# Light experts of a top-2-of-8 MoE layer as plain fp32 matmuls on two 64-column tiles of the array

## The chip, the core and the metric

One core of a Trainium2 chip runs the whole program. The metric is the device time in microseconds (us) of one execution; the profile gives the time from the first to the last instruction (the span) of one profiled execution. TensorE (PE) multiplies and transposes, ScalarE (ACT) and VectorE (DVE) work on SBUF and on PSUM, SyncE (SP) issues nearly all DMAs. Weights are read from HBM, each byte once.

## The reference, cut to what matters

The model is a trunk of two layers with 256 tokens of width 1024. The mixers and the dense feed-forward of layer 0 stay as they are. The change is in the channel mixer of layer 1:

```
def swiglu(h, wg, wu, wd):
    return (jax.nn.silu(h @ wg) * (h @ wu)) @ wd

def moe_top2(h, router, wg, wu, wd):          # h: 256 tokens x 1024; wg, wu: 8 x 1024 x 3584; wd: 8 x 3584 x 1024
    logits = (hf @ router).astype(jnp.float32)
    top_val, top_idx = lax.top_k(logits, TOP_K)          # 2 of 8 experts for each token
    gates = jax.nn.softmax(top_val, axis=-1)
    ...                                                  # tokens sorted by expert, padded to blocks of 128
    return swiglu(xblk, wg[e], wu[e], wd[e])             # for each block; times the gate, added back to the tokens
```

Everything is fp32. With 8 experts of 3 x 1024 x 3584 weights the layer reads 352 MB.

## The kernel before

**Units.** The weights of an expert are cut into 42 units of 1 MB (128 partitions x 2048 fp32): 28 units of gate and up weights (`c` below `DOWN0`), then 14 units of down weights. They are read into a ring of `SLOTS` = 7 buffers, `ring`. SP waits until the unit 7 places earlier has been used by PE, then issues the load of the next (L1322, in `beside`).

**Hi and lo.** PE has a fast pass for fp32 data rounded to a shorter form (written fp32r). To keep the accuracy, each unit is split: ACT writes the rounded part to `w_hi` (`moe_split` of ACT, L1431), DVE writes the rest, the raw unit minus that, to `ring_lo` (`moe_split` of DVE, L1950). Both run `MOE_LEAD` = 4 units ahead of PE. A product is then made of hi x hi, hi x lo and lo x hi.

**Heavy and light experts.** The 8 experts are sorted by the number of their tokens. The heavy one of a pair has up to 128 tokens, the light one up to 64 (`LIGHT`). Four pairs are worked off. For a heavy expert the tokens are the stationary operand, 128 columns, and each 512 weights of a row are streamed three times (`product`, L570 to L572): 12 matmuls of 512 columns in a unit. For a light expert the 64 tokens stand twice in the 128 columns of the array, once as hi and once as lo (`xl_both`, `elT_both`), and each 512 weights are streamed twice, once from `w_hi` and once from `ring_lo` (L1055, L1056 in `in_unit`; L1080, L1081 in `down_unit`): 8 matmuls in a unit. The result lies in PSUM in two halves of 64 partitions that have to be added. This is done with the transposition that the hidden layer needs anyway: ACT copies 1024 columns from PSUM to SBUF (`light_take`), and PE multiplies each 128 columns with `fold`, two identities of 64 under one another (`transposed`, L1110; `light_gT` and `light_uT` call it, 14 times with four matmuls for each light expert, 13 of them in a light half and the last at the start of the next heavy half). Silu and the product of gate and up follow on the transposed data (`light_silu`, `light_gated`), and a hi/lo split of that (`light_hi`, `light_rest`).

**Order.** The order is written out by hand. A pair has two halves of 42 units. In the heavy half (`heavy_up`) two units of the gate and up weights of the heavy expert are followed by one down unit of the light expert before it; in the light half (`light_up`) two gate and up units of the light expert are followed by one down unit of the heavy one. The first heavy half has only its 28 heavy units. After the last light half come 14 down units of the last light expert (`light_down`), and then the rest of the layer. Within the halves lie the gathering of tokens (`gather`, L988), transposes of the heavy hidden layer (`heavy_hidden`, L1104) and the scattering of results to the tokens (`scatter`, L995, plain fp32), each at a fixed unit.

The lines that the steps of the prediction touch are L570 to L572, L1055, L1056, L1080, L1081 and L1110 on PE, L1431 on ACT, L1950 on DVE and L1322 on SP.

Of the kernel before, what the change touches and what calls it, by code (L numbers as in the profile page):

```python
# [36 lines left out]
P = 128  # L37
# [56 lines left out]
PAIR_UNITS = 2 * EXPERT_UNITS  # L94

# [23 lines left out]
def trunk(nc, params, x, p, positions, w_in, w_uq, w_ukv, w_out, dense_g, dense_u, dense_d, router,  # L119
          moe_g, moe_u, moe_d, ple_g, ple_p, final_g, out):  # L120
    with ExitStack() as ctx:
# [48 lines left out]
        class View:  # L170
# [83 lines left out]
        xl = xT_r[:, 0:KT * 2 * LIGHT].rearrange("p (k r s) -> p k r s", k=KT, r=2)  # L254
        xl_both = [xl[:, kt].rearrange("p r s -> p (r s)") for kt in range(KT)]
        vx = View(xT_b, KT * 2 * LIGHT, 2 * NT * D)
        sgT, hx = vx(8 * LIGHT), vx(8 * LIGHT)
        light_y = vx(D)
        el_at1 = vx.at
        el_at0 = vf.at  # L260
        el_at3 = el_at0 + 16 * LIGHT
        vf.at = el_at3 + 8 * LIGHT
        light_selgT, fold = vf(NT * P), vf(LIGHT)

        elT = [buf[:, at:at + 2 * n * LIGHT].rearrange("p (k r s) -> p k r s", k=n, r=2) for buf, at, n in (
            (arena_b_r, el_at0, 8), (xT_r, el_at1, 8), (small_r, 0, 8), (arena_b_r, el_at3, 4))]
        elT_both = [elT[kt // 8][:, kt % 8].rearrange("p r s -> p (r s)") for kt in range(FKT)]
# [60 lines left out]
        moe_x_hi, heavy_h_hi, light_h_hi = sem("moe_x_hi"), sem("heavy_h_hi"), sem("light_h_hi")  # L328
# [26 lines left out]
        class Banks:  # L355
# [35 lines left out]
        sgT_ready, uT_full, hx_ready = (sem(n) for n in ("sgT_ready", "uT_full", "hx_ready"))  # L391
        selgT_full, selgT_ready = sem("selgT_full"), sem("selgT_ready")
        gT_full, lT_free = sem("gT_full"), sem("lT_free")
        hT_full, hT_free, d_full, ysb_ready, sc_full, sc_free, xg_full, xg_free, consts_ready = (sem(n) for n in (
            "hT_full", "hT_free", "d_full", "ysb_ready", "sc_full", "sc_free", "xg_full", "xg_free",
            "consts_ready"))

        MOE_USED = EXPERT_UNITS - len(GROUP_ENDS)
        HT_FILLS = FKT // 4
        SCATTER = (4, 7, 4, 7)  # L400
        LAST_SCATTER = (4, 7, 0, 1)


        def position(k, c):


            up, half = c < DOWN0, EXPERT_UNITS if (c < DOWN0) == (k == 1) else 0
            return half + (c // 2 * 3 + c % 2 if up else 3 * (c - DOWN0) + 2)

        def round_of(i, k, c):  # L410

            return i + 1 if k and c >= DOWN0 else i

        def is_start(i, k, c):

            return isinstance(i, int) and i == 0 and k == 0 and c < DOWN0

        def counted_used(k, c):

            return sum(1 for kk in range(2) for cc in range(EXPERT_UNITS)  # L420
                       if position(kk, cc) <= position(k, c) and cc not in GROUP_ENDS)

        START_USED = sum(1 for c in range(DOWN0) if c not in GROUP_ENDS)

        def ch_done(i, k, ch):
            return i * (2 * NCH) + k * NCH + ch + 1

        def hT_done(i, k, n):
            return i * (NCH if k else HT_FILLS) + n + 1
# [4 lines left out]
        def xg_done(i, k, half=0):  # L434
            return i * 3 + 2 * k + half + 1

        def d_done(i, k, half):
            return i * 4 + 2 * k + half + 1
# [8 lines left out]
        def unit_of(i, k, c):  # L447

            if is_start(i, k, c):
                return S0 + c  # L450
            return round_of(i, k, c) * PAIR_UNITS + S0 - DOWN_UNITS + position(k, c)

        def ring_of(k, c, start=False):

            return N0 + c if start else N0 - DOWN_UNITS + position(k, c)

        def tail_of(n_iter, j):

            return n_iter * PAIR_UNITS + S0 - DOWN_UNITS + j

        def after_of(n_iter, c):

            return n_iter * PAIR_UNITS + S0 + c


        def by_cols(w, c0, n=SEQ):

            return [(w.rearrange("(k p) n -> p k n", p=P)[:, :, c0:c0 + n], KT, n)]
# [52 lines left out]
        def turn(g, in_moe=False):  # L521
            return S0 + g - N0 if in_moe or g >= N0 else TURN[g]
# [4 lines left out]
        def high(g, n=UNIT, in_moe=False):  # L527
            a = turn(g, in_moe) % HIGHS * UNIT
            return w_hi[:, a:a + n]

# [13 lines left out]
        def _(pe):  # L544
# [435 lines left out]
            def gather(i, k, kt):  # L980
# [8 lines left out]
                if kt % per_bank == per_bank - 1:  # L989
                    last.then_inc(xg_full, 1)  # L990

            def scatter(k, n, b, first, final):

                t, half = divmod(n, 2)
                last = mm(psum[:, b, :], selgT[k][:, t, :], ysb[k][:, half * 512:half * 512 + 512],  # L995
                          start=first, stop=final)
                if final:
                    last.then_inc(sc_full, 1)

            def scatter_two(i, n):  # L1000
# [3 lines left out]
                if n == 0:  # L1004
                    pe.wait_ge(selgT_ready, step_done(i, 0))
                    pe.wait_ge(ysb_ready, d_done(i, 0, 1))
                elif n == 2:
                    pe.wait_ge(selgT_ready, step_done(i, 1))
                    pe.wait_ge(ysb_ready, d_done(i, 1, 1))
                if n < 2:  # L1010
                    pe.wait_ge(hT_free, hT_done(i + 1, 0, n))
                else:
                    pe.wait_ge((sgT_ready, hx_ready)[n - 2], (i + 1) * NCH + 1)
# [4 lines left out]
            def spread_gates(i, k, b=7):  # L1018

                pe.wait_ge(selg_ready, step_done(i, k))  # L1020
                if b != 7:
                    pe.wait_ge(ysb_ready, d_done(i, 0, 1))
# [1670 lines left out]
```

## Time and profile before

| | us |
|---|---|
| median of 3 runs (lowest to highest) | 1483.17 (1481.64 to 1484.45) |
| span of the profiled execution | 1481.2 |
| PE matmul, busy | 1439.9 (97%) |
| PE weight load, busy | 1190.4 (80%) |
| DVE, busy | 1216.5 (82%) |
| ACT, busy | 1026.3 (69%) |
| the 336 expert units, from the first matmul to the last | about 890 |

Busy times are sums of the records of an engine. The record of a matmul begins when it starts to stream and ends when its last result is modelled to have left the array, so records of one stream overlap: what a matmul costs in a stream is the distance between two starts, not its own length. A row of the timeline with xN joins N records. One plain fp32 matmul is two MATMUL records, an fp32r matmul is one. An "idle before" in square brackets is time in which that engine had nothing running, and the name behind the arrow is what ended it.

### The profile page before, as it was taken

To read this page: it belongs to the slowest core of one execution; us is meant where nothing else is said; L and a number is where in the kernel's file an instruction comes from. 1 tells how busy PE (TensorE), PEld (TensorE's weight loads), DVE (VectorE), ACT (ScalarE), POOL (GpSimd) and SP (SyncE) were. 2 spreads that over 40 slices of the span, in tenths; PEclk is the share of its full clock that TensorE was granted. 3 is DMA by queue.
4 is the path that set the end of the run, shared out by engine and by line. 5 is a ranking of instruction groups with operands and counts; after the bars stand their busy time and mean duration, and the time that the engine had idled before them with its cause. 6 is when DMAs were issued, how large, how long until landed. Compare 5 with 4: busy or idle time off the path is not lost.

```text
span 1481.2 us, 18816 instructions
## 1 busy us (share of the span) xinstructions
PE 1439.9 (97%) x7071; PEld 1190.4 (80%) x7071; DVE 1216.5 (82%) x1125; ACT 1026.3 (69%) x949; POOL 6.9 (0%) x14
## 2 busy tenths in 40 slices
PE   7999999999899999999999999999999999999997
PEld 6878888888797777887888878887878887878875
DVE  6996644653589878999999999989899989899995
ACT  6566452441645658788887878877788887788885
POOL 0000000000000000000000000000000000000000
PEclk9999999999999999999999999999999999999999
DMA  9415555556542039999999999999999999999991
GB/s 324 157 57 168 198 175 195 181 188 199 161 143 86 8 143 411 395 393 410 401 381 402 390 400 406 401 380 389 390 397 409 402 381 385 397 399 409 400 403 73
DMA packets 143962, 443.93 MB, mean 300 GB/s; under 512 B 6961, under 2 KB 21329, under 8 KB 143617
## 3 DMA queue, kind: packets, MB, share of 16 engines
q1 hardware_dynamic: 142976, 439.29, 78.7%
q0 software_dynamic: 896, 3.44, 0.6%
q8 instruction: 57, 0.93, 0.2%
q14 instruction: 33, 0.26, 0.0%
HBM read 440.61 MB, written 2.10 MB: 299 GB/s over the span
## 4 chain that ended last, share of the span: by engine, by line
PE 84%; DMA 6%; DVE 6%; ACT 3%; issue 1%; SPq 0%; DVEq 0%; ACTq 0%
PE psum L570 18%; PE psum L572 18%; PE psum L571 18%; PE psum L1055 5%; PE psum L1056 5%; DMA ring<-in_moe_w_down 3%; PE psum L1110 3%; PE psum L1080 3%; PE psum L1081 3%; PE psum L612 2%; PE psum L995 2%; PE psum L591 2%; PE psum L988 1%; DVE ring_lo L1950 1%; DMA ring<-in_moe_w_gate 1%; ACT w_hi L1431 1%
## 5 line engine op out<-in xcount | busy, mean ns | idle before, releaser
L1950 DVE TENSOR_TENSOR ring_lo<-ring,w_hi 128x2048 fp32r<-128x2048 f32 x336 | 762.1, 2289 | 66.3 <-ACT w_hi L1431 63.1
L1431 ACT ACTIVATE w_hi<-ring 128x2048 fp32r<-128x2048 f32 x336 | 641.8, 1918 | 139.2 <-DMA ring<-in_moe_w_gate 53.9
L1944 DVE TENSOR_TENSOR ring_lo<-ring,w_hi 128x2048 fp32r<-128x2048 f32 (+1 forms) x71 | 159.4, 2267 | 105.3 <-ACT w_hi L1425 105.2
L572 PE MATMUL psum<-w_hi,hidden_b 128*128 128x512 f32 x560 | 218.5, 390 | 0.0
L1055 PE MATMUL psum<-w_hi,xT_parts 128*128 128x512 f32 x448 | 179.4, 401 | 0.5 <-DVE ring_lo L1950 0.3
L570 PE MATMUL psum<-w_hi,hidden_b 128*128 128x512 f32 x448 | 178.3, 398 | 1.5 <-DVE ring_lo L1944 1.4
L1056 PE MATMUL psum<-ring_lo,xT_parts 128*128 128x512 f32 x448 | 174.9, 390 | 0.0
L571 PE MATMUL psum<-ring_lo,hidden_b 128*128 128x512 f32 x448 | 174.5, 390 | 0.0
L1425 ACT ACTIVATE w_hi<-ring 128x2048 fp32r<-128x2048 f32 (+1 forms) x71 | 132.0, 1898 | 31.5 <-PE psum L572 27.8
L570 PE MATMUL psum<-w_hi,xT_parts 128*128 128x512 f32 (+1 forms) x384 | 149.5, 389 | 1.3 <-DVE xT_parts L1957 1.0
L572 PE MATMUL psum<-w_hi,xT_parts 128*128 128x512 f32 (+1 forms) x384 | 148.5, 387 | 0.0
L571 PE MATMUL psum<-ring_lo,xT_parts 128*128 128x512 f32 (+1 forms) x384 | 148.3, 386 | 0.0
L570 PE MATMUL psum<-w_hi,hidden_a 128*128 128x512 f32 x352 | 142.9, 406 | 4.8 <-DVE ring_lo L1950 4.7
L571 PE MATMUL psum<-ring_lo,hidden_a 128*128 128x512 f32 x352 | 137.2, 390 | 0.0
L572 PEld LDWEIGHTS psum<-w_hi,hidden_b 128*128 128x128 f32 x560 | 105.1, 188 | 22.6
L570 PEld LDWEIGHTS psum<-w_hi,hidden_b 128*128 128x128 f32 x448 | 84.2, 188 | 20.3 <-DVE ring_lo L1944 2.3
L1055 PEld LDWEIGHTS psum<-w_hi,xT_parts 128*128 128x128 f32 x448 | 84.3, 188 | 18.9 <-DVE ring_lo L1950 2.8
L571 PEld LDWEIGHTS psum<-ring_lo,hidden_b 128*128 128x128 f32 x448 | 84.2, 188 | 17.6 <-issue 0.7
L1056 PEld LDWEIGHTS psum<-ring_lo,xT_parts 128*128 128x128 f32 x448 | 84.2, 188 | 16.2
L572 PE MATMUL psum<-w_hi,hidden_a 128*128 128x512 f32 x240 | 93.9, 391 | 0.0
L570 PEld LDWEIGHTS psum<-w_hi,hidden_a 128*128 128x128 f32 x352 | 66.2, 188 | 23.5 <-DVE ring_lo L1950 8.4
L570 PEld LDWEIGHTS psum<-w_hi,xT_parts 128*128 128x128 f32 x384 | 72.1, 188 | 15.1 <-issue 1.7
(336 smaller groups left out, 1874.1 us busy)
## 6 DMA issues: line engine op xcount, KB each, us to landing
ring<-in_moe_w_gate SPq DMA_DIRECT2D x112, 1024.0 KB, 8.4
ring<-in_moe_w_up SPq DMA_DIRECT2D x112, 1024.0 KB, 8.7
ring<-in_moe_w_down SPq DMA_DIRECT2D x112, 1024.0 KB, 8.8
ring<-in_w_in SPq DMA_DIRECT2D x16, 1024.0 KB, 5.4
ring<-in_dense_w_gate SPq DMA_DIRECT2D x14, 1024.0 KB, 5.1
ring<-in_dense_w_up SPq DMA_DIRECT2D x14, 1024.0 KB, 5.1
ring<-in_dense_w_down SPq DMA_DIRECT2D x14, 1024.0 KB, 4.9
ring<-in_w_out SPq DMA_DIRECT2D x8, 1024.0 KB, 4.9
```

The source lines that it names most:

```text
L570: mm(o, a[0], b[0], start=first, stop=False)
L571: mm(o, a[0], b[1], start=False, stop=False)
L572: return mm(o, a[1], b[0], start=False, stop=final)
L1055: mm(o, xl_both[kt], w[0][:, q, cols], start=kt == 0, stop=False)
L1056: last = mm(o, xl_both[kt], w[1][:, q, cols], start=False, stop=kt == KT - 1)
L1080: mm(o, elT_both[kt], w[0][:, q, cols], start=kt == 0, stop=False)
L1081: last = mm(o, elT_both[kt], w[1][:, q, cols], start=False, stop=kt == FKT - 1)
L1110: last = mm(psum[:, b, q * LIGHT:q * LIGHT + LIGHT], src[:, q * P:q * P + P], fold, start=True, stop=True)
L1425: A(high(g, sizes[g]), raw(g, sizes[g]), ACT.Copy).then_inc(hi_ready, 1)
L1431: A(high(g, in_moe=True), raw(g), ACT.Copy).then_inc(hi_ready, 1)
L1944: V.tensor_tensor(low(g, sizes[g]), raw(g, sizes[g]), f32(high(g, sizes[g])), ALU.subtract).then_inc(lo_ready, 1)
L1950: V.tensor_tensor(low(g), raw(g), f32(high(g, in_moe=True)), ALU.subtract).then_inc(lo_ready, 1)
```

## The change

For light experts the split is given up. The 64 tokens stand as one stationary operand of 64 columns in plain fp32 (`xl`, `elT`), and the raw unit in the ring is streamed in plain fp32. The function `halves_of` sends the first 512 weights of a row to PSUM partitions 0 to 63 and the other 512 to partitions 64 to 127. The two matmuls thereby stand in two tiles of the array, each 128 rows by 64 columns. In the units of the last, shorter chunk of gate and up it is 256 weights each.

```
+            def halves_of(b, x, w, n, first, final):
+                for half in range(2):
+                    last = mm(psum[half * LIGHT:half * LIGHT + LIGHT, b, 0:n], x, w[:, half * n:half * n + n],
+                              start=first, stop=final)
+                return last
+            def light_in(i, c):
+                ch = c // 8
+                kts, n = (2, 512) if ch < NCH - 1 else (4, 256)
...
+                pe.wait_ge(loaded[g % SLOTS], landed(g, i))
...
+                for q in range(kts):
+                    kt = kts * r + q
+                    last = halves_of((LIGHT_G, LIGHT_U)[u][ch], xl[:, kt, :], w[:, q, :], n, kt == 0, kt == KT - 1)
+                last.then_inc((lg_full, lu_full)[u] if r == units - 1 else light_used, 1)
...
+            def light_down(i, j, tail=False):
...
+                for q in range(2):
+                    kt = 2 * j + q
+                    last = halves_of(2 if tail else 5, elT(kt), w[:, q, :], 512, kt == 0, kt == FKT - 1)
...
+            def light_hidden(i, ch):
...
+                for q in range(4 if ch < NCH - 1 else 2):
+                    last = tr(psum[:, 4, q * P:q * P + P], light_h[:, q * P:q * P + P], ident)
+                last.then_inc(lT_full, 1)
```

Gate and up of a light chunk now fill one PSUM bank each, 128 partitions x 512. Silu (`light_silu`) and the product (`light_gated`) work on them as they are, and `light_hidden` transposes the product: 4, 4, 4 and 2 transposes for a light expert. `light_take`, `light_gT`, `light_uT`, `transposed`, `fold`, the light `take_light` and `light_rest` of DVE are gone. `light_hi` is now one plain copy.

```
-                mm(o, xl_both[kt], w[0][:, q, cols], start=kt == 0, stop=False)
-                last = mm(o, xl_both[kt], w[1][:, q, cols], start=False, stop=kt == KT - 1)
...
-            def moe_split(g, i, wait):
+            def moe_split(i, c, g, landing):
-                act.wait_ge(loaded[g % SLOTS], landed(g, i))
-                act.wait_ge(*wait)
-                A(high(g, in_moe=True), raw(g), ACT.Copy).then_inc(hi_ready, 1)
+                act.wait_ge(loaded[g % SLOTS], landing)
+                act.wait_ge(*high_reader(i, c))
+                A(heavy_high(c), raw(g), ACT.Copy).then_inc(hi_ready, 1)
...
+                    def split_at(i, half, p):
...
+                        k, c = ROUND[half][p]
+                        if k == 0:
+                            g = ring_of(half, p)
+                            moe_split(i, c, g, landed(g, i))
```

ACT and DVE split only the units of heavy experts (`k == 0`). PE waits for the landing of a light unit itself. The order of the units stays: two up units of one expert, one down unit of the other (`GROUP` = 2, `ROUND`), and so do the ring, its 7 slots and the loads. The light part of a scatter reads 64 rows in place of 128, because the light result lies in two halves of partitions:

```
+                if k:
+                    rows = slice(half * LIGHT, half * LIGHT + LIGHT)
+                    last = mm(psum[:, b, :], selgT[k][rows, t, :], light_y[rows, :], start=first, stop=final)
```

On PE, before, in the first light half, around two light units between the second chunk's folds (L1110; `hidden_a` is the hidden layer of the heavy expert, `xT_parts` the light tokens): a light unit is eight matmuls, L1055 and L1056 in turn, and a fold call stands before, between and behind the two.

```order
L571 MATMUL psum<-ring_lo,hidden_a 128x512
L572 MATMUL psum<-w_hi,hidden_a 128x512
L1110 MATMUL psum<-arena_b 128x64 x4
L1055 MATMUL psum<-w_hi,xT_parts 128x512
L1056 MATMUL psum<-ring_lo,xT_parts 128x512
...
L1110 MATMUL psum<-arena_b 128x64 x4
L570 MATMUL psum<-w_hi,hidden_a 128x512
```

On PE, now, in the same half, with one transposition of the light hidden layer (L1159) ahead of two light units (L1094):

```order
L580 MATMUL psum<-ring_lo,hidden_a 128x512
L581 MATMUL psum<-w_hi,hidden_a 128x512
L1159 MATMUL psum<-par,xT 128x128 x4
L1094 MATMUL psum<-ring,xT 64x512 x8
L579 MATMUL psum<-w_hi,hidden_a 128x512
```

The three fold calls are gone, and sixteen full-array matmuls of two units have become eight plain fp32 matmuls of 64 columns that read the raw ring and follow one another directly.

On PE, before, in a heavy half, the first light down unit (L1080, L1081) between two heavy units:

```order
L571 MATMUL psum<-ring_lo,hidden_b 128x512
L572 MATMUL psum<-w_hi,hidden_b 128x512
L1110 MATMUL psum<-arena_b 128x64 x4
L1080 MATMUL psum<-w_hi,hidden_b 128x512
L1081 MATMUL psum<-ring_lo,hidden_b 128x512
...
L570 MATMUL psum<-w_hi,hidden_b 128x512
```

On PE, now, at such a place:

```order
L580 MATMUL psum<-ring_lo,hidden_b 128x512
L581 MATMUL psum<-w_hi,hidden_b 128x512
L1094 MATMUL psum<-ring,xT 64x512 x4
L579 MATMUL psum<-w_hi,hidden_b 128x512
L580 MATMUL psum<-ring_lo,hidden_b 128x512
```

The light unit has four matmuls, two in each tile, and the array goes from its full width to two tiles and back around it. There are 14 such places in each half.

## Rows read from the trace of the kernel before

**Rows 1.** The page: span, busy time of the engines (share, instructions).
```profile
span 1481.2 us, 18816 instructions
PE 1439.9 (97%) x7071; PEld 1190.4 (80%) x7071; DVE 1216.5 (82%) x1125; ACT 1026.3 (69%) x949; POOL 6.9 (0%) x14
```

**Rows 2.** Stretches: us, busy us of PE, PEld, DVE, ACT, POOL (instructions), clock, DMA share, GB/s.
```profile
557.00:632.00 75.00, 73.94 (x335) 60.50 (x335) 67.51 (x36) 59.18 (x39) 0.58 (x1) 1.00 1.02 401
632.00:742.50 110.50, 108.10 (x537) 88.99 (x535) 102.06 (x57) 90.09 (x60) 0.00 (x0) 1.00 1.02 401
742.50:853.80 111.30, 111.30 (x520) 91.82 (x519) 104.81 (x63) 88.62 (x59) 0.00 (x0) 1.00 1.02 392
853.80:965.00 111.20, 109.85 (x546) 90.76 (x544) 102.34 (x57) 91.06 (x63) 0.00 (x0) 1.00 1.02 402
965.00:1077.00 112.00, 112.00 (x519) 91.72 (x518) 104.01 (x62) 88.03 (x59) 0.00 (x0) 1.00 1.01 387
...
1411.00:1447.00 36.00, 35.15 (x143) 24.85 (x142) 32.23 (x22) 27.39 (x23) 0.00 (x0) 1.00 1.02 399
```

**Rows 3.** Groups by line: busy us, mean ns of one, idle before, releaser.
```profile
L1950 DVE TENSOR_TENSOR ring_lo<-ring,w_hi 128x2048 fp32r<-128x2048 f32 x336 | 762.1, 2289 | 66.3 <-ACT w_hi L1431 63.1
L1431 ACT ACTIVATE w_hi<-ring 128x2048 fp32r<-128x2048 f32 x336 | 641.8, 1918 | 139.2 <-DMA ring<-in_moe_w_gate 53.9
```

**Rows 4.** Waits: who waited for whom, us in total, times, longest.
```profile
PE psum L570 <- DVE ring_lo L1950: 4.7, 9, 0.7
```

**Rows 5.** Timeline of PE, two light units, one heavy, a transposition: start us, length us.
```profile
853.79 0.39 PE L1055 MATMUL psum<-w_hi,xT_parts 128*128 128x512 f32 x1
854.01 0.39 PE L1056 MATMUL psum<-ring_lo,xT_parts 128*128 128x512 f32 x1
...
857.41 0.39 PE L570 MATMUL psum<-w_hi,hidden_a 128*128 128x512 f32 x1
...
860.14 0.60 PE L1104 MATMUL psum<-par,arena_b 128*128 128x128 f32 x4
860.50 0.48 PE L1055 MATMUL psum<-w_hi,xT_parts 128*128 128x512 f32 x1
860.81 0.39 PE L1056 MATMUL psum<-ring_lo,xT_parts 128*128 128x512 f32 x1
```

**Rows 6.** Timeline of PE, one fold and two plain fp32 scatter matmuls.
```profile
1116.38 1.00 PE L1110 MATMUL psum<-arena_b 128*128 128x64 f32 x8
1117.19 0.48 PE L1055 MATMUL psum<-w_hi,xT_parts 128*128 128x512 f32 x1
1117.50 0.39 PE L1056 MATMUL psum<-ring_lo,xT_parts 128*128 128x512 f32 x1
...
1119.12 1.02 PE L995 MATMUL psum<-arena_b 128*128 128x512 f32 x2
1119.98 1.02 PE L995 MATMUL psum<-xT,arena_b 128*128 128x512 f32 x2
1120.43 0.80 PE L570 MATMUL psum<-w_hi,hidden_a 128*128 128x512 f32 x1
1121.07 0.40 PE L571 MATMUL psum<-ring_lo,hidden_a 128*128 128x512 f32 x1
```

**Rows 7.** Timeline of PE's weight loads: one load of 128 columns.
```profile
801.24 0.19 PEld L571 LDWEIGHTS psum<-ring_lo,hidden_b 128*128 128x128 f32 x1
```

**Rows 8.** Timeline of ACT where DMA sets the pace of the splits.
```profile
872.43 1.92 ACT L1431 ACTIVATE w_hi<-ring 128x2048 fp32r<-128x2048 f32 x1 [0.37 <-DMA ring<-in_moe_w_up]
875.00 1.92 ACT L1431 ACTIVATE w_hi<-ring 128x2048 fp32r<-128x2048 f32 x1 [0.65 <-DMA ring<-in_moe_w_down]
877.56 1.92 ACT L1431 ACTIVATE w_hi<-ring 128x2048 fp32r<-128x2048 f32 x1 [0.64 <-DMA ring<-in_moe_w_gate]
880.12 1.92 ACT L1431 ACTIVATE w_hi<-ring 128x2048 fp32r<-128x2048 f32 x1 [0.64 <-DMA ring<-in_moe_w_gate]
```

**Rows 9.** The end of the last light expert: timelines of ACT, DVE and PE.
```profile
1435.56 1.92 ACT L1431 ACTIVATE w_hi<-ring 128x2048 fp32r<-128x2048 f32 x1 [0.38 <-DMA ring<-in_moe_w_down]
1437.51 2.29 DVE L1950 TENSOR_TENSOR ring_lo<-ring,w_hi 128x2048 fp32r<-128x2048 f32 x1 [0.28 <-ACT w_hi L1431]
1439.85 0.50 PE L1080 MATMUL psum<-w_hi,hidden_b 128*128 128x512 f32 x1 [0.46 <-DVE ring_lo L1950]
```

More of the change, by code:

```diff
@@ L401, in trunk @@
         LAST_SCATTER = (4, 7, 0, 1)
[L404 to L429, printed above, removed]
+        LIGHT_G, LIGHT_U = (1, 0, 1, 0), (3, 2, 3, 2)
+        def position(c):
+            if c < DOWN0:
+                return c // GROUP * GROUP_ALL + c % GROUP
+            j = c - DOWN0
+            return j // GROUP_DOWN * GROUP_ALL + GROUP + j % GROUP_DOWN
@@ new lines, in unit_at, with is_start, ch_done @@
+        def unit_at(half, p):
+            n, r = divmod(p, GROUP_ALL)
+            if r < GROUP:
+                return half, n * GROUP + r
+            return 1 - half, DOWN0 + n * GROUP_DOWN + r - GROUP
+        ROUND = [[unit_at(half, p) for p in range(EXPERT_UNITS)] for half in range(2)]
+        assert all(position(c) == p for half in range(2) for p, (k, c) in enumerate(ROUND[half]))
+        def is_start(i, c):
+            return isinstance(i, int) and i == 0 and c < DOWN0
+        def ch_done(i, ch):
+            return i * NCH + ch + 1
@@ L1147, in heavy_up @@
             def heavy_up(i):
                 behind = not (isinstance(i, int) and i == 0)
[L1151 to L1152 removed]
+                for k, c in ROUND[0]:
+                    if k:
+                        if behind:
+                            light_down(i - 1, c - DOWN0)
+                        continue
+                    heavy_in(i, c)
                     if c in (9, 17, 25):
@@ L1197, in light_down @@
-            def light_down(i):
+                for k, c in ROUND[1]:
+                    if k:
+                        light_in(i, c)
+                        if c in (25, 26) and not last:
+                            if c == 25:
+                                pe.wait_ge(lg_free, ch_done(i, 2))
+                            else:
+                                pe.wait_ge(lu_free, ch_done(i, 2))
+                            for kt in range(4):
+                                gather(i + 1, 0, kt + 4 * (c - 25))
+                        continue
+                    j = c - DOWN0
+                    heavy_down(i, j)
+                    if j == 0:
+                        heavy_hidden(i, 6)
+                    elif j == 1 and behind:
+                        spread_gates(i - 1, 1)
+                    elif j in (3, 7, 11, 13):
+                        light_hidden(i, (3, 7, 11, 13).index(j))
+                    elif j in (5, 9) and behind:
+                        scatter_two(i - 1, 2 + (j - 5) // 4)
+                    if j == 11:
+                        spread_gates(i, 0)
@@ L1267, in _, with count_used, heavy_reader @@
                             last_x(1)
-                    if i == 0:
-                        last.then_inc(unit_used, 1)
             used_before_moe.append(used[0])
-        def moe_reader(i, k, c):
+        def count_used(c):
+            return sum(1 for n in range(c + 1) if n not in GROUP_ENDS)
+        def heavy_reader(i, c):
             if c == EXPERT_UNITS - 1:
-                return d_full, d_done(i, k, 1)
+                return d_full, d_done(i, 1)
             if c in GROUP_ENDS:
@@ L1801, in light_up @@
                     def light_up(i, last=False):
                         behind = not (isinstance(i, int) and i == 0)
-                        for c in range(DOWN0):
-                            if c == 0 and behind:
-                                take_y(i - 1, 1)
-                            elif c == 2:
+                        for p, (k, c) in enumerate(ROUND[1]):
+                            before = ROUND[1][p - 1] if p else None
+                            if p == 0 and behind:
+                                take_light_y(i - 1)
+                            if before == (0, DOWN0):
```

666 lines of the change are left out of this document (289 added, 377 removed).

## The prediction

> **What bounds the kernel now.** I read the table of stretches first, then PE's timeline, then the waits, and DMA last. The expert layer fills about 890 of the 1481.2 us [rows 1, 2]: one start of 28 heavy units (75 us), four light halves (110.5 to 111.2 us), three heavy halves (111.3 to 112 us) and a tail of 14 units (36 us). In the halves PE is busy from 97.8 to 100%, and its waits for DVE's lo parts on heavy matmuls are 4.7 us in the whole run [rows 2, 4]. So PE sets the pace. Its plain work confirms it: a light unit is 8 matmuls, and two of them take 857.41 − 853.79 = 3.62 us, 0.227 us a matmul and 1.82 us a unit; the heavy unit behind takes 860.14 − 857.41 = 2.73 us [rows 5]. A heavy half is then 28 x 2.73 + 14 x 1.82 = 101.9 us, and scatters, gathers and transposes fill the other 9.4. DVE (2.29 us a unit) and ACT (1.92 us) have room at 2.65 us a unit [rows 3].
>
> DMA is close behind. Where ACT waits for each load, its splits start 2.56 us apart (875.00, 877.56, 880.12) [rows 8], and that is the pace of the transfers. 42 units at 2.56 us are 107.5 us. No half can be shorter than that, since the change moves the same bytes. So at most 3.6 us can be won in a half of 111.1 us.
>
> **The change part by part.**
>
> *Splits of light units.* 168 x 2.29 = 385 us of DVE and 168 x 1.92 = 323 us of ACT go away [rows 3]. They lie beside PE's stream and are worth only what PE waits, about 1 us in a light half [rows 2]. In the tail they are on the path: the last light unit is taken up by ACT at 1435.56 and by PE at 1439.85 [rows 9]. Without the splits PE starts 4.3 us earlier and the unit is 0.3 longer (below): −4 us, once.
>
> *Folds.* A fold call takes 0.81 us and the next matmul 0.31 in place of 0.227, 0.9 us in all [rows 6]. 13 of them leave a light half (−11.9), 1 leaves a heavy half (−0.9). Four transposes of the light hidden layer come in, priced at 0.36 + 0.09 = 0.45 us by L1104 [rows 5]: +1.8 us in a light half.
>
> *The light unit itself.* No row shows a 64-column tile. What rows show is plain fp32 on the full array: two records, 0.86 us for one matmul of 512 columns, 0.43 us a record [rows 6]. A light unit now issues 4 matmuls, 8 records. The bounds are 8 x 0.43 = 3.44 us if the tiles do not overlap at all, and 1.72 us if both run side by side all the time. I take neither. Starts on PE are in order in every row that I read; a matmul's two records must follow each other in their tile; so of A1 A2 B1 B2 (A in one tile, B in the other) only B1 can start with A2, and the next A1 with B2. Four matmuls then take five steps, 5 x 0.43 = 2.15 us, and two units in a row nine steps, 3.87 us. Against 1.82 and 3.64 that is +0.33 x 14 = +4.6 us in a heavy half and +0.23 x 14 = +3.2 us in a light half. (The units of the short chunk have 16 records of half the length, and come out 0.2 us lower; I leave that.) By this the change costs PE time in a heavy half, where little is removed.
>
> *Going from full width to tiles and back.* 28 times in a half, and 4 times more for the light scatters, which now stand on 64 rows. The change from plain fp32 to fp32r costs nothing: two scatter matmuls from 1119.12 are over at 1120.84 at 0.43 a record, and 1121.07 − 0.227 is 1120.84 [rows 6]. After transposes and folds it is 0.09 us. That is the lower bound if tiles are like any other change of form. The upper bound is an array that has to run empty and be loaded anew: a record is 0.39 us long at a distance of 0.227, so 0.16 us for the last results to leave, and 0.19 us for a weight load [rows 5, 7], 0.35 us. I take 0.16 us, the emptying alone, since loads run ahead of the matmuls everywhere else. 32 x 0.16 = 5.1 us in a half. The Trainium skill says it outright (TensorEngine Tiling (Array Packing), Key Properties): changing the tiling mode drains the TensorE, while changing the tile within a mode does not. No row here shows it. By that page the 5.1 us stand; by the scatter rows they would be nothing and the result would fall on the other side of zero (first rival).
>
> *Waits.* PE now waits itself for the landing of a light unit, with the next heavy units and SP's load 7 places on queued behind it. Before, ACT needed each load 4 units ahead of PE, so the landing is early for PE: nothing. The 8 loads around a light unit, the slots and SP's waits are as before.
>
> *Sum.* Heavy half: +4.6 − 0.9 + 5.1 = +8.8 us, three times: +26.4. Light half: PE's own work is 111.1 less about 1.5 us of waits, 109.6; 109.6 + 3.2 − 11.9 + 1.8 + 5.1 = 107.8, which is also what DMA allows (107.5): −3.3 us, four times: −13.2. Start: unchanged. Tail: −4. In all +9 us on a span of 1481.2, so 1490.5; the median of the runs was 2.0 above the span: 1492.5, I say 1493.
>
> **The rivals.**
>
> *The change of tiling is free (faster).* Then a heavy half has +4.6 − 0.9 = +3.7 (three times 11), a light half falls to DMA's 107.5 (−3.6, four times −14.4), and with the tail −4 the sum is −7 us: 1476. For it speaks the free change from fp32 to fp32r. It decides at about 0.11 us a switch: below, the kernel is faster than before. If in addition both tiles start together, a light unit is 1.72 us, a heavy half 2.3 us shorter than before and the sum −25 us: 1458. Against this speaks the order of the records.
>
> *A weight load is exposed at each step (slower).* Eight folds of 128 columns take 0.81 us, 0.10 each, although they stream only 64 columns: there the load is the limit [rows 6]. For 64 columns half of that, 0.05 us, could lie between steps if loads do not run ahead for both tiles at once: four times in a lone unit, eight in two: +2.8 us in a heavy half and +5.6 in a light one. Sum: 3 x 11.6 + 4 x (113.4 − 111.1) − 3.5 = +40 us: 1523. The forecast's own case with switches of 0.35 us gives 3 x 14.9 + 4 x 2.8 − 3 = +53: 1536; with 0.09 us it gives +2: 1485.
>
> *The tiles do not overlap (much slower).* 3.44 us a light unit: heavy half +22.7 − 0.9 + 5.1 = +26.9, light half 109.6 − 51.0 + 96.3 − 11.9 + 1.8 + 5.1 = 149.9, which is +38.8, tail 14 x 3.44 + 4 against 36, +16: about +250 us: 1735. The code places the tiles at different partitions of PSUM, so nothing in the order forbids the overlap, but no row shows it either. The Trainium skill (TensorE: Matmul & The Clock Gate, Part 3) reports column tiles running concurrently, 2.38 times for three tiles of 32 columns, and matmuls that start and end in program order; the first speaks against this rival, the second is what my steps assume. Neither is seen in this trace.
>
> **How the numbers follow.** Forecast (tiles overlap with one step lost, switches cost 0.09 to 0.35 us): 0.42, own range 1485 to 1536. Free switches: 0.33. Both tiles at once as well: 0.05. Exposed weight loads: 0.10. No overlap: 0.10. The range leaves out the last and part of the 1458: 1466 to 1536. What a measurement can tell from no change is 0.2%, 3 us. Faster: 0.29 of the free switches and the 0.05, 0.34. Same: the rest of the free switches and the cheap end of the forecast, 0.10. Slower: 0.36 + 0.10 + 0.10 = 0.56.
>
> **What would show it.** In PE's timeline of the new kernel: records of L1094 at 0.43 us if they are serial, at 0.215 on average if they overlap, in pairs that start together after the first. From the last fp32r start before a light unit to the first one after it: 0.227 + 2.15 + 0.32 us in a heavy half by my forecast, 2.38 with free switches. Light halves of 107.5 to 108 us with ACT or PE waiting for DMA, heavy halves of 120 us with DMA below 380 GB/s. Splits x168 with the same lengths. The last light unit's matmuls right behind its landing. I am wrong if heavy halves stay near 111 us, or if light halves are over 115. The clock should stay at full speed throughout, as it is in every stretch now [rows 2]; if short waits brought it down, all sums would be too low.

## The result and the profile after

The changed kernel takes 1531.82 us (median of 4 runs, 1531.26 to 1534.05) against 1482.67 us (4 runs, 1481.64 to 1484.45): 1.0332 times as long, with a 95% interval of 1.0319 to 1.0346. The forecast was 1493 and the range 1466 to 1536. The direction is right and the size is not: +49 us in place of +10. That 1531.8 lies inside the range is luck: its upper end, 1536, stood for tile switches of 0.35 us each, and these were not what cost the time.

The page after, first its head and then the split groups (busy us, mean ns of one, idle before):

```profile
span 1529.4 us, 17485 instructions
PE 1437.5 (94%) x6807; PEld 992.6 (65%) x6807; DVE 833.6 (55%) x936; ACT 687.7 (45%) x745; POOL 6.9 (0%) x14
...
L1936 DVE TENSOR_TENSOR ring_lo<-ring,w_hi 128x2048 fp32r<-128x2048 f32 x168 | 383.9, 2290 | 450.2 <-ACT w_hi L1434 450.2
...
L1434 ACT ACTIVATE w_hi<-ring 128x2048 fp32r<-128x2048 f32 x168 | 321.5, 1915 | 407.8 <-DMA ring<-in_moe_w_down 248.3
```

PE has as much busy time as in [rows 1], within 2.4 us, in a span that is 48.2 us longer. The splits are halved and as long as in [rows 3]. So the time went into waiting. The table of stretches says where (us, busy us of PE, PEld, DVE, ACT, POOL with instructions, clock, DMA share, GB/s):

```profile
549.80:632.50 82.70, 80.41 (x362) 64.94 (x361) 69.80 (x37) 61.56 (x41) 0.58 (x1) 1.00 1.03 402
632.50:752.70 120.20, 104.36 (x478) 56.00 (x477) 41.94 (x29) 36.56 (x28) 0.00 (x0) 0.91 0.96 366
752.70:866.70 114.00, 114.00 (x512) 75.99 (x512) 68.54 (x43) 57.77 (x39) 0.00 (x0) 1.00 1.01 385
866.70:987.70 121.00, 108.10 (x488) 56.80 (x485) 44.15 (x30) 37.55 (x30) 0.00 (x0) 0.94 0.97 367
987.70:1104.00 116.30, 116.30 (x517) 76.52 (x517) 68.10 (x43) 57.67 (x39) 0.00 (x0) 1.00 1.00 377
...
1458.40:1491.00 32.60, 31.81 (x130) 9.58 (x128) 0.80 (x1) 3.88 (x6) 0.00 (x0) 1.00 1.02 399
```

Rows 2 and 4 of this table are light halves. They have grown where [rows 2] have 110.5 and 111.2, with PE idle for 15.8 and 12.9 us, a clock of 0.91 and 0.94, and DMA at 366 GB/s where it ran at 401. The heavy halves (rows 3 and 5) have no idle time. Cut at the first matmul of the first unit of each half in both traces:

| stretch | before | after | difference | forecast |
|---|---|---|---|---|
| 4 light halves | 438.6 | 479.6 | +41.0 | −13.2 |
| 3 heavy halves | 337.1 | 346.3 | +9.2 | +26.4 |
| tail, 14 units | 33.65 | 32.49 | −1.2 | −4 |
| ahead of them and behind | 671.8 | 671.0 | −0.8 | 0 |
| span | 1481.2 | 1529.4 | +48.2 | +9 |

In the kernel before the tail begins here:

```profile
1408.19 0.48 PE L1080 MATMUL psum<-w_hi,hidden_b 128*128 128x512 f32 x1
```

The row of 36 us in [rows 2] starts at 1411.0, one unit into the tail, and runs 5 us past its last unit. Measured from 1408.2, the fourth light half of before is 107.1 us long, where the prediction took 110.5 to 111.2 for all four.

### The profile page after: what moved, and what is told of

Read it like the earlier page. It is cut to its first block, busy times and chain, and to the rows that moved or that the text cites. A ratio compares the mean times of both kernels' runs of the same rounds, so it can differ in the third digit from the quotient of the medians.

```text
span 1529.4 us, 17485 instructions
## 1 busy us (share of the span) xinstructions
PE 1437.5 (94%) x6807; PEld 992.6 (65%) x6807; DVE 833.6 (55%) x936; ACT 687.7 (45%) x745; POOL 6.9 (0%) x14
## 3 DMA queue, kind: packets, MB, share of 16 engines
q0 software_dynamic: 896, 3.44, 0.6%
## 4 chain that ended last, share of the span: by engine, by line
PE 80%; DMA 9%; DVE 5%; ACT 3%; issue 3%; SPq 0%; DVEq 0%; ACTq 0%
PE psum L1094 18%; PE psum L579 18%; PE psum L580 17%; PE psum L581 17%; DMA ring<-in_moe_w_down 6%; PE psum L621 2%; ACT w_hi L1434 2%; PE psum L600 2%; PE psum L997 1%; DMA ring<-in_moe_w_gate 1%; PE psum L1008 1%; PE psum L639 1%; PE psum L1006 1%; PE psum L1148 1%; DVE arena_a L2017 1%
## 5 line engine op out<-in xcount | busy, mean ns | idle before, releaser
L1936 DVE TENSOR_TENSOR ring_lo<-ring,w_hi 128x2048 fp32r<-128x2048 f32 x168 | 383.9, 2290 | 450.2 <-ACT w_hi L1434 450.2
L1434 ACT ACTIVATE w_hi<-ring 128x2048 fp32r<-128x2048 f32 x168 | 321.5, 1915 | 407.8 <-DMA ring<-in_moe_w_down 248.3
L1094 PE MATMUL psum<-ring,xT 128*64 128x512 f32 (+1 forms) x1472 | 330.8, 592 | 0.0
L581 PE MATMUL psum<-w_hi,hidden_b 128*128 128x512 f32 x560 | 218.5, 390 | 0.0
L1094 PEld LDWEIGHTS psum<-ring,xT 128*64 128x64 f32 x1472 | 102.3, 145 | 178.2 <-issue 171.8
L579 PE MATMUL psum<-w_hi,hidden_b 128*128 128x512 f32 x448 | 182.7, 408 | 1.6 <-DVE ring_lo L1930 1.2
L579 PE MATMUL psum<-w_hi,xT_parts 128*128 128x512 f32 (+1 forms) x384 | 149.5, 389 | 1.3 <-DVE xT_parts L1941 1.0
L581 PE MATMUL psum<-w_hi,xT_parts 128*128 128x512 f32 (+1 forms) x384 | 148.5, 387 | 0.0
L579 PE MATMUL psum<-w_hi,hidden_a 128*128 128x512 f32 x352 | 144.1, 409 | 1.3 <-DVE ring_lo L1936 1.1
L581 PEld LDWEIGHTS psum<-w_hi,hidden_b 128*128 128x128 f32 x560 | 105.1, 188 | 23.3
L579 PEld LDWEIGHTS psum<-w_hi,hidden_b 128*128 128x128 f32 x448 | 84.1, 188 | 52.6 <-issue 21.2
L579 PEld LDWEIGHTS psum<-w_hi,hidden_a 128*128 128x128 f32 x352 | 66.0, 188 | 54.4 <-issue 36.0
L580 PEld LDWEIGHTS psum<-ring_lo,hidden_b 128*128 128x128 f32 x448 | 84.2, 188 | 15.8 <-issue 0.2
L581 PE MATMUL psum<-w_hi,hidden_a 128*128 128x512 f32 x240 | 93.7, 390 | 0.0
L579 PEld LDWEIGHTS psum<-w_hi,xT_parts 128*128 128x128 f32 x384 | 72.1, 188 | 15.1 <-issue 1.7
L581 PEld LDWEIGHTS psum<-w_hi,xT_parts 128*128 128x128 f32 x384 | 72.1, 188 | 14.1
L580 PEld LDWEIGHTS psum<-ring_lo,xT_parts 128*128 128x128 f32 x384 | 72.1, 188 | 13.4
```

The costliest lines, as they stand in the source:

```text
L579: mm(o, a[0], b[0], start=first, stop=False)
L580: mm(o, a[0], b[1], start=False, stop=False)
L581: return mm(o, a[1], b[0], start=False, stop=final)
L1094: last = mm(psum[half * LIGHT:half * LIGHT + LIGHT, b, 0:n], x, w[:, half * n:half * n + n], start=first, stop=final)
L1434: A(heavy_high(c), raw(g), ACT.Copy).then_inc(hi_ready, 1)
L1936: V.tensor_tensor(low(g), raw(g), f32(heavy_high(c)), ALU.subtract).then_inc(lo_ready, 1)
```

## The wait in the light halves

The table of waits of after (who waited for whom, us, times, longest) has an entry that before does not have:

```profile
ACT w_hi L1434 <- DMA ring<-in_moe_w_down: 248.3, 51, 9.0
...
PE psum L1159 <- DVE xT L2401: 54.4, 12, 5.8
```

L1159 holds the transposes of the product of gate and up (`light_hidden`), and L2401 is that product on DVE (`light_gated`). There are three such waits in each light half. One of them, on PE (start us, length us, idle before and its releaser):

```profile
886.84 3.65 PE L1094 MATMUL psum<-ring,xT 128*64 128x512 f32 x16
...
898.97 1.12 PE L1159 MATMUL psum<-par,xT 128*128 128x128 f32 x4 [5.28 <-DVE xT L2401]
900.02 5.85 PE L1094 MATMUL psum<-ring,xT 128*64 128x512 f32 x16
```

and on ACT and DVE:

```profile
894.08 1.91 ACT L1434 ACTIVATE w_hi<-ring 128x2048 fp32r<-128x2048 f32 x1 [5.78 <-DMA ring<-in_moe_w_down]
```
```profile
888.34 2.29 DVE L1936 TENSOR_TENSOR ring_lo<-ring,w_hi 128x2048 fp32r<-128x2048 f32 x1 [5.38 <-ACT w_hi L1434]
896.02 2.29 DVE L1936 TENSOR_TENSOR ring_lo<-ring,w_hi 128x2048 fp32r<-128x2048 f32 x1 [5.40 <-ACT w_hi L1434]
898.23 0.68 DVE L2401 TENSOR_TENSOR xT<-psum,xT 128x512 f32<-128x512 f32 x1
```

DVE had nothing to do from 890.6 to 896.0, yet the product, 0.68 us long, ran only at 898.23. It stood in DVE's queue behind the lo split of a heavy unit that PE needs 4 units later. That split waited for ACT's hi split, and this for the landing of its load. Now that only one load in three is split in a light half, two unsplit loads land between two splits, and a split that looks ahead waits 5 to 6 us for its data where in [rows 8] it waited about 0.65. Whatever stands behind it in the queue waits as long. In the kernel before, the product of a chunk was not queued when its last unit was done, but some light units later (at `c` = 11, 19 and 27, for the chunk that ended at 7, 15 and 23), and what used it was later again.

The stall brings two costs after it. Four stretches in a row, from the last busy microseconds before the stall (same columns as above):

```profile
893.00:899.00 6.00, 0.72 (x5) 0.26 (x3) 2.98 (x3) 1.91 (x1) 0.00 (x0) 0.89 1.03 410
899.00:902.00 3.00, 3.00 (x10) 1.44 (x12) 0.43 (x2) 0.83 (x2) 0.00 (x0) 0.50 1.02 408
902.00:905.00 3.00, 3.00 (x10) 0.83 (x10) 1.29 (x1) 1.67 (x1) 0.00 (x0) 0.59 0.39 111
905.00:908.00 3.00, 3.00 (x16) 1.80 (x11) 1.00 (x1) 0.00 (x0) 0.00 (x0) 1.00 0.91 315
```

After 5.3 us without a matmul the granted clock is at 0.50, half of full speed (the level of 1.2 GHz). By the last three rows it stays there until about 904.5, 5.5 us after the matmuls went on, and the 16 records behind take 5.85 us in place of 3.65. PE frees no buffers while it stands, so SP issues no load from 894.1 to 903.7, and DMA falls to 111 GB/s in 902 to 905.

## Experiments: the wait

**e1_gated_first**: the product goes ahead of the split in DVE's queue, and nothing else is changed.

```
-                        elif before in ((1, 7), (1, 15), (1, 23), (1, 27)):
-                            light_gated(i, before[1] // 8)
...
+                        if (k, c) in ((1, 7), (1, 15), (1, 23), (1, 27)):
+                            light_gated(i, c // 8)      # ahead of split_at(i, 1, p + MOE_LEAD)
```

> The changed kernel, with one thing moved on DVE: in a light half the product of gate and up of the light expert is queued ahead of the lo split of the heavy unit four places on, and no longer behind it. Theory Q (queue): the product was late because the split ahead of it on DVE waited for ACT, and ACT for a load that PE needs only four units later; PE stood 3.6 to 5.8 us at each of 12 transposes, and 2 to 3 us more went each time the clock fell. Then 12 x about 4.6 = 55 us go, and what is saved is bounded by DMA at 2.56 us a unit: light halves 107.5 to 109 us, heavy halves unchanged at 114 to 116, in all 1474 to 1484 us. Theory T (tiles): the time went into tile switches and 64-column matmuls; then the product's place changes nothing, 1525 to 1535 us. Theory D (DMA): loads come late by themselves, and PE waits at the next unit instead: also over 1515 us.

Measured: 1485.21 us (1482.34 to 1487.13, 10 runs), 1.0018 times before (1.0008 to 1.0028). Of the 49 us, 46.6 are gone, as theory Q has it; the time is 1.2 us above its range. DVE in e1:

```profile
877.47 2.29 DVE L1936 TENSOR_TENSOR ring_lo<-ring,w_hi 128x2048 fp32r<-128x2048 f32 x1 [5.38 <-ACT w_hi L1434]
879.84 0.69 DVE L2401 TENSOR_TENSOR xT<-psum,xT 128x512 f32<-128x512 f32 x1
885.14 2.29 DVE L1936 TENSOR_TENSOR ring_lo<-ring,w_hi 128x2048 fp32r<-128x2048 f32 x1 [4.61 <-ACT w_hi L1434]
```

DVE still waits 4.6 us for the hi split, but the product starts 5.3 us ahead of the split that it would have stood behind. PE's transposes start without a wait, at full speed, and the whole wait is 3.0 us in the run:

```profile
882.69 0.60 PE L1159 MATMUL psum<-par,xT 128*128 128x128 f32 x4
883.22 3.65 PE L1094 MATMUL psum<-ring,xT 128*64 128x512 f32 x16
```
```profile
PE psum L1159 <- DVE xT L2401: 3.0, 2, 1.6
```

A light and a heavy half of e1:

```profile
855.70:964.50 108.80, 103.76 (x488) 56.23 (x485) 42.39 (x29) 34.89 (x29) 0.00 (x0) 0.98 1.03 405
964.50:1080.60 116.10, 116.10 (x514) 76.43 (x515) 69.83 (x44) 59.78 (x41) 0.00 (x0) 1.00 1.00 380
```

Against the light half of after at 866.7 the idle time falls from 12.9 to 5.0 us and PE's busy time from 108.1 to 103.8, while the clock goes from 0.94 to 0.98: 12.2 us together, all of the difference. All four light halves come to 431.4 us, 7.2 less than before; the heavy ones stay at 346.3. What PE waits for now is the lo split of heavy units, 24.6 us in 28 waits, behind ACT's split and this behind the load:

```profile
PE psum L579 <- DVE ring_lo L1936: 24.6, 28, 1.9
```

**e2_hidden_later**: DVE's queue is left as it is, and PE transposes a chunk one down unit later (two light units and one heavy unit).

```
-                    elif j in (3, 7, 11, 13):
-                        light_hidden(i, (3, 7, 11, 13).index(j))
+                    elif j in (4, 8, 12, 13):
+                        light_hidden(i, (4, 8, 12, 13).index(j))
```

> The changed kernel, with PE's transposes of the light hidden layer one heavy unit and two light units later for the first three chunks (and ACT's copy behind them moved likewise); DVE's queue is as it was. Theory Q: the product still comes 4 to 5 us late, but PE has 6.4 us of other work before it asks for it, so at least 10 of the 12 stalls go and it comes within 5 us of the kernel with the product first: 1474 to 1488 us. Theory T: 1525 to 1535. Theory D: over 1515.

Measured: 1486.70 us (1484.13 to 1489.42, 7 runs), ratio 1.0024 (1.0012 to 1.0035). That is in the range of theory Q. The wait of L1159 is 4.9 us. The cure from the other end gives nearly the same. So it was not the length of the product, the transposes or the lo split that cost the time, but that PE needed the product while it stood behind a split with later use.

## Experiments: the tiles

**What a light unit costs.** The forecast rested on the claim that of A1 A2 B1 B2 only B1 can start with A2, five steps for a lone unit. A lone unit of after, and inside it its first two records:

```profile
765.58 0.39 PE L581 MATMUL psum<-w_hi,hidden_b 128*128 128x512 f32 x1
765.90 1.94 PE L1094 MATMUL psum<-ring,xT 128*64 128x512 f32 x8
767.77 0.50 PE L579 MATMUL psum<-w_hi,hidden_b 128*128 128x512 f32 x1
```
```profile
765.90 0.65 PE L1094 MATMUL psum<-ring,xT 128*64 128x512 f32 x2
```

All 8 records start in pairs: 765.899 and .905, 766.379 and .385, 766.808 and .814, 767.237 and .244. Four steps, 1.87 us to the next heavy matmul. No step is lost. From L581 to L579 it is 767.77 − 765.58 = 2.19 us, where the forecast had 2.70 and free switches with a lost step 2.38.

**e4_one_tile** (on e1): all light matmuls of the first and of the second 512 weights into the same tile.

```
-                    last = mm(psum[half * LIGHT:half * LIGHT + LIGHT, b, 0:n], x, w[:, half * n:half * n + n],
-                              start=first, stop=final)
+                    last = mm(psum[0:LIGHT, b, 0:n], x, w[:, half * n:half * n + n],
+                              start=first and half == 0, stop=final and half == 1)
```

> The kernel with the product first, but both halves of a light unit go to the same 64 columns of the array and to the same 64 partitions of PSUM, so the light experts' results are left wrong; the number and form of matmuls is unchanged. If the two tiles overlap fully in the changed kernel (records in pairs 0.006 us apart, 4 steps of 0.43 us in a unit), a light unit goes from 1.8 to 3.44 us: heavy half about +23 us, light half about +42 from 107.5 to 150, tail +16, in all 1710 to 1735 us. If the 64-column form itself were quick and the second tile not needed, it stays below 1600.

Measured: 1735.9 us (one run). A lone light unit:

```profile
801.76 0.39 PE L581 MATMUL psum<-w_hi,hidden_b 128*128 128x512 f32 x1
802.08 3.65 PE L1094 MATMUL psum<-ring,xT 128*64 128x512 f32 x8
805.66 0.50 PE L579 MATMUL psum<-w_hi,hidden_b 128*128 128x512 f32 x1
```

3.58 us instead of 1.87. The eight records start 0.43 us apart, one after the other: the upper bound of the forecast (3.44), and the total is the 1735 of the rival without overlap, 0.9 us above the range expected here. With two tiles the second runs entirely beside the first.

**e7_tile_order** (on e1): PE's queue holds A A' B B' in place of A B A' B'. If starts were in the order of the queue, B could not begin before A' had.

```
-                for q in range(kts):
-                    kt = kts * r + q
-                    last = halves_of((LIGHT_G, LIGHT_U)[u][ch], xl[:, kt, :], w[:, q, :], n, kt == 0, kt == KT - 1)
+                for half in range(2):
+                    for q in range(kts):
+                        kt = kts * r + q
+                        last = half_of(half, (LIGHT_G, LIGHT_U)[u][ch], xl[:, kt, :], w[:, q, :], n, kt == 0, kt == KT - 1)
```

> The kernel with the product first, with the four matmuls of a light unit in another order: both of the left tile, then both of the right (A A' B B' in place of A B A' B'). The trace shows A and B starting 0.006 us apart although each is two records. If PE starts matmuls only in order and at most one per tile, B must wait for the second A' to start: 6 steps of 0.43 us in place of 4, a unit of about 2.6 us: +12 us a heavy half, light half from 108.5 to about 124, tail +5, in all 1570 to 1600 us. If PE looks ahead by tile, the unit stays at 1.8 us and the time at 1485.

Measured: 1491.59 us (one run).

```profile
763.50 0.39 PE L581 MATMUL psum<-w_hi,hidden_b 128*128 128x512 f32 x1
763.82 1.94 PE L1093 MATMUL psum<-ring,xT 128*64 128x512 f32 x8
765.69 0.50 PE L579 MATMUL psum<-w_hi,hidden_b 128*128 128x512 f32 x1
```
```profile
763.82 0.66 PE L1093 MATMUL psum<-ring,xT 128*64 128x512 f32 x2
```

Still 1.87 us, and the first two records start 0.013 us apart. Records of one tile do not overlap (e4), so the second must be of B, started before A'. The claim of the prediction falls. But the order is loosened by little. In a unit of the short chunk the queue of e7 holds four matmuls of A, then four of B, each of two records of 256 columns. Such a unit in e7, then in e1, where A and B take turns:

```profile
732.45 2.86 PE L1093 MATMUL psum<-ring,xT 128*64 128x256 f32 x16
```
```profile
731.58 1.95 PE L1094 MATMUL psum<-ring,xT 128*64 128x256 f32 x16
```

In e1 all 16 records start in pairs. In e7 four records start alone, about 0.22 us apart, then pairs follow, and the last four are alone again; the unit takes 2.79 us in place of 1.88. So the first matmul of B starts with the third of A: it has overtaken the fourth, and not the second and third. In both forms of unit B overtakes one matmul and no more; what sets this limit is not shown. The Trainium skill says that matmuls start and end in program order (TensorE: Matmul & The Clock Gate, Part 3); the trace of e7 does not agree where the matmuls are in different tiles. The Trainium skill also says that tiles operate independently (TensorEngine Tiling (Array Packing), Key Properties); the 1.87 us agree with this, the 2.79 us show where it ends. The short units are also where the 6 us of e7 over e1 lie, as far as one run of e7 can tell. The heavy halves, without units of the short chunk, are alike (346.2 and 346.3 us), and the light halves take 438.0 us against 431.4; the 16 short units cost PE about 10 us more there, of which the transfers can hide a part.

**What the switches cost.** Across a light unit in a heavy half the trace of after repeats every 7.57 us (one light and two heavy units, 765.90 to the next at 773.47). Without any switch it would be 24 x 0.227 + 4 x 0.43 = 7.17 us. One way in and out is thus 0.40 us, 0.20 us a switch; the forecast took 0.16 between bounds of 0.09 and 0.35. This can be tested by having fewer of them.

**e3_group4**: four units of one expert, then two of the other, by one constant (below) in the changed kernel. The number of switches is halved; what stands ahead of the transposes changes too.

```
-GROUP = 2
+GROUP = 4
```

> The changed kernel with four up units of one expert, then two down units of the other. It halves the number of tile switches and puts the product ahead of the blocking split in DVE's queue as a side effect. Theory Q: the stalls go and 14 fewer switch pairs in a heavy half of about 0.17 us each way give 2 to 3 us a heavy half more than the kernel with the product first: 1465 to 1480 us. Theory T: half of the 47 us, about 1507. If bursts of two light units starve on loads it is slower than the kernel with the product first.

Measured: 1478.03 us (1476.56 to 1480.11, 6 runs), ratio 0.9972 (0.9959 to 0.9984). Two light units in a row in a heavy half:

```profile
752.32 3.65 PE L1094 MATMUL psum<-ring,xT 128*64 128x512 f32 x16
755.90 0.50 PE L579 MATMUL psum<-w_hi,hidden_b 128*128 128x512 f32 x1
...
767.01 3.65 PE L1094 MATMUL psum<-ring,xT 128*64 128x512 f32 x16
```

Two light units take 3.58 us, against 3.62 in [rows 5], and 14.69 us for two light and four heavy units against 2 x 7.57 = 15.14. Half the switches save 0.45 us for six units, 0.23 a switch. The wait for the product has also gone (2.8 us are left). A heavy half has 7 ways in and out in place of 14 (the expectation speaks of 14 fewer pairs, and means 14 fewer switches). That makes 3 x 7 x 0.45 = 9.5 us; the three heavy halves take 337.9 us against 346.3 in e1, 8.4 less, and the two spans differ by 8.5. The light halves gain nothing by it (433.3 us against 431.4).

**e6_group4_first** (e3 with the edit of e1) has e3's order and the product ahead of the split.

> The group-of-four kernel with the product of gate and up also queued ahead of the split in the same step on DVE. With groups of four no heavy split stands between the last up unit of a chunk and its product, so theory Q expects no change: within 2 us of 1478. A gain of more than 3 us would mean that part of the queue was still blocking there.

Measured: 1476.36 us (1474.52 to 1479.58, 5 runs), ratio 0.9958 (0.9944 to 0.9972). It is the fastest kernel of this study, 5.7 us below before; against e3 the ranges overlap, so e1's edit has nothing more to give here.

**e5_before_group4**: the same order in the kernel before, written into its loops by hand (core of the edit):

```
-                        if c % 2:
-                            down_unit(i - 1, 1, c // 2)
+                        for j in ((c // 2 - 1, c // 2) if c % 4 == 3 else ()):
+                            down_unit(i - 1, 1, j)
```

> The kernel before (light experts with hi/lo split and fold) in the order of the group-of-four kernel: four up units of one expert, then two down units of the other. It tells whether that kernel owes its time to the tiles or to the order alone. If the order helps only by halving the tile switches, which this kernel does not have, it stays at 1481 to 1485 us. If the order itself is good for DMA or PE's waits, it comes to 1477 to 1480 too; if bursts starve it, over 1487.

Measured: 1485.58 us (1483.56 to 1487.56, 10 runs), ratio 1.0021 (1.0012 to 1.0031), 0.6 us above what was expected of an order that helps by switches alone. Without tiles the order gives nothing, and the heavy halves stay as they are (337.6 us against 337.1). What e3 and e6 gain over e1 comes from light units with half the switches.

## Experiments: the tail

In e6, behind the last light expert (PE, then ACT):

```profile
1439.11 1.99 PE L1006 MATMUL psum<-xT,arena_b 64*128 64x512 f32 x8 [1.68 <-ACT xT L1751]
1441.55 2.34 PE L600 MATMUL psum<-par,h 128*128 128x128 f32 x16 [0.44 <-DVE h L2413]
```
```profile
1436.57 1.91 ACT L1434 ACTIVATE w_hi<-ring 128x2048 fp32r<-128x2048 f32 x1 [7.45 <-DMA ring<-in_ple_w_gate]
1438.38 0.58 ACT L1751 ACTIVATE xT<-psum 128x512 f32<-128x512 f32 x1
```

The same pattern again: the copy of the results (L1751) behind a split with later use. **e8_tail_copy_first** (on e6) and **e9_group2_both** (on e1) put the copy first:

```
-                            if j == DOWN_UNITS - MOE_LEAD:
-                                after_split(i + 1, 0)
...
+                        after_split(i + 1, 0)      # behind take_light_y(i, 2)
```

> The kernel in groups of four with the product first, and on ACT at the end of the last light expert the copy of its result out of PSUM queued ahead of the hi split of the first gate unit of the next stage. In the kernel without this, ACT stands 7.5 us for that unit's load, and PE waits 1.7 us for the copy behind the split. By theory Q PE's wait goes and the time falls by 1 to 2.5 us, to 1474 to 1476. If the end is set by the loads of the next stage, whose split is now 0.6 us later, it stays within 0.5 us of 1476.4.

> The kernel with the product first in its own groups of two, with the same move of the copy at the tail. PE waited 2.4 us for that copy there. Theory Q: 1482.5 to 1484, the same as the kernel before within 0.2%. If loads set the end, 1485 as without it.

Measured: e8 1479.18 us (1475.84 to 1481.35, 11 runs), ratio 0.9976 (0.9967 to 0.9985); e9 1485.79 us (1482.94 to 1488.38, 10 runs), ratio 1.0020 (1.0010 to 1.0029). Nothing is gained in either: e1 had 1.0018, and the intervals of e6 and e8 overlap, with the median of e8 2.8 us the higher. e8 misses both of its forecasts, e9 misses that of theory Q and is where its rival had it. PE and DVE in e8:

```profile
1435.72 1.99 PE L1006 MATMUL psum<-xT,arena_b 64*128 64x512 f32 x8 [0.79 <-ACT xT L1751]
1440.45 3.48 PE L600 MATMUL psum<-par,h 128*128 128x128 f32 x16 [2.73 <-DVE h L2412]
```
```profile
1437.41 2.29 DVE L1935 TENSOR_TENSOR ring_lo<-ring,w_hi 128x2048 fp32r<-128x2048 f32 x1 [38.12 <-ACT w_hi L1434]
1439.62 2.47 DVE L2412 TENSOR_TENSOR h<-h,psum 128x512 f32<-128x512 f32 x4
```

PE waits 0.9 us less for the copy and 2.3 us more for the addition to `h`, which now stands on DVE behind the lo split of the same unit. The wait moved to the next queue that has the same fault. An edit that puts DVE's addition first as well was not tried.

## Why the prediction was right or wrong, point by point

**Splits of light units: right outside the tail.** 168 are left, as long as before, and their removal bought nothing by itself.

**Tail, −4 us: wrong, −1.2 in after and +0.5 in e1.** The step took the 4.3 us from ACT's split to PE's first matmul of the last unit for time on the path. But PE was busy with the units ahead of it until shortly before: the bracket in [rows 9] says that it stood for 0.46 us. PE's last five units in after, and the wait for the copy of the results behind them:

```profile
1481.36 8.80 PE L1094 MATMUL psum<-ring,xT 128*64 128x512 f32 x40
1490.95 1.99 PE L1006 MATMUL psum<-xT,arena_b 64*128 64x512 f32 x8 [0.79 <-ACT xT L1751]
```

There is no pause from 1458.5 on, and the last load landed at 1484.45, 3.8 us before PE took it up. So PE's own work sets the end, not the splits and not the loads. That work is 31.7 us in after and in e1, against 32.8 before (33.65 less waits of 0.39 and 0.46). In e1 the wait for the copy is 2.42 us in place of 0.79, and the tail 34.13 us.

**The light unit, one step lost: wrong.** It was priced at 2.15 us of steps, and four steps of 0.43 are 1.72. This term made +4.6 us of each heavy half and +3.2 of PE's work in each light one; it is −1.4 and −2.8 instead (14 x and 28 x (1.72 − 1.82)). The rival that both tiles start together had 0.05.

**Switches, 0.16 us each: right in kind, a little low** (0.20 by the 7.57-us period, 0.23 by e3, in both with the change of number format in it). Free switches, the rival with 0.33, are refuted by both; so is an exposed weight load at each step, for steps within a unit stand 0.43 us apart. With both terms set right a heavy half is −1.4 − 0.9 + 14 x 0.40 = +3.3 us, and measured are +2.7, +3.3 and +3.3. The forecast of 8.8 had 6.0 too much for the lost step and 0.5 too little for the switches, in three halves 16.5 of the 17.2 us that it was off. (The 4 switches at scatters, which its 5.1 us has, were not measured by themselves.) The prediction says that the result turns at 0.11 us a switch; by its own terms 3 x (3.7 + 32 x s) − 14.4 − 4 is zero for a switch s of 0.08 us.

**Light halves bound by DMA at 107.5 us: right in e1, hidden in after.** The Sum gave 107.8; e1 has 107.9 on average (431.4 / 4) with DMA at 405 GB/s and a share of 1.03. The 107.8 for PE had the lost step in it; without it PE's work is about 102 us, and the transfers alone make the 107.9. So the error of the step did no harm here. "No half can be shorter" is too strict: the fourth takes 105.6 us in e1, and 40 loads, not 42, landed in it.

**Waits, "nothing": the step that failed.** It looked only at how early each load lands for PE. It did not ask what stands in the queues of DVE and ACT behind a split that now waits longer, although the change itself moved the product of gate and up up to the place where it is used at once, and behind such a split. This one step is 54.4 us of stalls. It makes up the whole difference between after and e1, 44.1 us of span (48.2 in the light halves): the stalls and the slow clock after them, less what PE then waits for the transfers. The forecast named the sign, light halves over 115 us, and the loss of clock as a danger for all sums; both came. It gave neither a chance nor a price.

**The sum, corrected.** Of e1's span, 4.1 us above before's, +9.2 are in the heavy halves, −7.2 in the light ones, +0.5 in the tail and +1.7 ahead of them and behind. The forecast of +9 was near this by errors that cancel in part, which is luck: 17.2 us too much in the heavy halves, against 4.5 too little in the tail, 6.0 in the light halves (it set out from 111.1 us, where the four of before are 109.7 on average) and 1.7 elsewhere. The change as written cost 44 us more, by the place of one instruction of 0.68 us.

## What to carry to other kernels

When work is taken away from an in-order queue, look at what remains in it: operations that look ahead wait longer for their data, and all that stands behind them waits too, urgent or not. Put what the busiest engine needs next ahead of what it needs units later, and follow such an edit into each queue along the chain, since the wait moves to the next one. Where a form of work needs a switch of the array, put units of one form together; here half of the switches turned +0.2% into −0.4%.

## What the runs showed of the hardware

- Two tiles of 128 rows by 64 columns run plain fp32 fully side by side: 1.87 us for 8 records against 3.58 in one tile, with starts 0.006 us apart.
- PE started a matmul ahead of one of the other tile that stood before it in the queue, and of one only: with two matmuls of A ahead of B the unit still takes 1.87 us (starts 0.013 us apart, e7), with four it takes 2.79 in place of 1.88.
- Between fp32r on the full array and plain fp32 on two tiles, in and out cost 0.40 us together, where the change between the two number formats alone showed none [rows 6].
- In a stall of 5.3 us without a matmul the granted clock fell to 0.50 and was still there 5.5 us after the matmuls went on; 16 records took 5.85 us in place of 3.65. It fell around each of the 12 stalls (3.6 to 5.8 us long).
